# A two-layer decoder trunk on one core: one weight block's low part moves from VectorE to GpSimd, and its high part one place back on ScalarE

## The reference

```python
def one_block(args):            # forgetting attention
    sc = jnp.einsum('bqhd,bkhd->bhqk', qi, k) * scale
    sc = sc + ci[..., None] - logcum[:, :, None, :]
    sc = jnp.where(mask[None, None], sc, -jnp.inf)
    p = jax.nn.softmax(sc, axis=-1)
    return jnp.einsum('bhqk,bkhd->bqhd', p.astype(v.dtype), v)
...
y = jnp.concatenate([mix, mo], axis=-1) @ w_o[layer]
x = layer_norm(DN_ALPHA * x + y, ln_g[layer, 0], ln_b[layer, 0])
x = layer_norm(DN_ALPHA * x + sq_relu_mlp(x, w_up[layer], w_down[layer]),
               ln_g[layer, 1], ln_b[layer, 1])
```

## Time and profile before

| | |
|---|---|
| median of 3 runs | 1163.6 us (1163.14 to 1164.12) |
| profiled execution | 1163.3 us |
| its span, first to last instruction | 1161.6 us |
| TensorE busy | 1139.0 us, 98% |
| VectorE busy | 623.5 us, 54% |
| ScalarE busy | 487.4 us, 42% |
| GpSimd busy | 131.6 us, 11% |
| last forgetting step, units 0 to 7 on TensorE | about 734.6 to 751.8 us of the span |

### The profile page before, as it was taken

The page is one execution under the profiler, slowest core; times in us unless marked ns, Lnnn a source line. Parts: engine busy times, 40 slices in busy tenths (PEclk is TensorE's granted clock), DMA queues, the critical chain, the costliest instruction groups (busy, mean ns, idle before and its releaser), DMA issues.

```text
span 1161.6 us, 16344 instructions
## 1 busy us (share of the span) xinstructions
PE 1139.0 (98%) x5792; PEld 960.9 (83%) x5792; DVE 623.5 (54%) x1065; ACT 487.4 (42%) x843; POOL 131.6 (11%) x157
## 2 busy tenths in 40 slices
PE   8999999999999999999999999999999999999997
PEld 7888889888888888889778888788888888888886
DVE  6668766444223444355587787746454233444226
ACT  6556358343122343225765656537443212334120
POOL 5000054000000000233301101046000000000000
PEclk9999999999999999999999999999999999999999
DMA  8222323233333333332212222133233333333232
GB/s 308 77 73 91 100 65 109 74 106 92 103 97 91 92 105 93 103 96 82 65 39 71 55 55 72 41 105 92 80 100 95 105 90 90 91 92 106 91 112 88
DMA packets 163798, 107.22 MB, mean 92 GB/s; under 512 B 4642, under 2 KB 156194, under 8 KB 163620
## 3 DMA queue, kind: packets, MB, share of 16 engines
q1 hardware_dynamic: 163172, 104.18, 29.8%
q10 hardware_dynamic: 576, 2.36, 0.6%
HBM read 104.43 MB, written 2.10 MB: 92 GB/s over the span
## 4 chain that ended last, share of the span: by engine, by line
PE 85%; DVE 6%; ACT 4%; issue 2%; DMA 2%; POOL 1%; SPq 0%; DVEq 0%; ACTq 0%; POOLq 0%
PE proj L581 69%; PE pv L581 3%; PE sc L581 2%; PE proj L976 2%; PE sc L976 2%; PE pv L976 2%; PE tr L976 2%; PE tr L632 1%; DVE w_lo L1585 1%; ACT w_hi L1193 1%; DMA w_raw<-in_w_o 1%; PE proj L676 1%; DVE sc L1654 1%; DMA mem_raw<-in_mem 1%; ACT x L1376 0%
## 5 line engine op out<-in xcount | busy, mean ns | idle before, releaser
L581 PE MATMUL proj<-x_hi,w_hi 128*128 128x512 f32 (+1 forms) x752 | 291.7, 389 | 3.5 <-DVE w_lo L1585 1.6
L1585 DVE TENSOR_TENSOR w_lo<-w_raw,w_hi 128x1024 fp32r<-128x1024 f32 (+1 forms) x168 | 210.0, 1251 | 155.1 <-ACT w_hi L1193 107.1
L581 PE MATMUL proj<-x_hi,w_lo 128*128 128x512 f32 (+1 forms) x752 | 287.1, 383 | 0.0
L581 PE MATMUL proj<-x_lo,w_hi 128*128 128x512 f32 (+1 forms) x752 | 282.6, 383 | 0.0
L1193 ACT CAST w_hi<-w_raw 128x1024 fp32r<-128x1024 f32 x153 | 159.9, 1045 | 203.2 <-PE proj L581 199.6
L581 PEld LDWEIGHTS proj<-x_hi,w_hi 128*128 128x128 f32 x752 | 141.4, 188 | 31.2 <-ACT x_hi L1378 2.8
L581 PEld LDWEIGHTS proj<-x_hi,w_lo 128*128 128x128 f32 x752 | 141.3, 188 | 28.2
L581 PEld LDWEIGHTS proj<-x_lo,w_hi 128*128 128x128 f32 x752 | 139.2, 188 | 24.9
L581 PE MATMUL proj<-h_hi,w_hi 128*128 128x512 f32 (+1 forms) x384 | 146.4, 381 | 0.4 <-DVE w_lo L1585 0.4
L581 PE MATMUL proj<-h_hi,w_lo 128*128 128x512 f32 (+1 forms) x384 | 146.1, 380 | 0.0
L581 PE MATMUL proj<-h_lo,w_hi 128*128 128x512 f32 (+1 forms) x384 | 146.0, 380 | 0.0
(11 more groups left out here) (380 smaller groups left out, 1784.1 us busy)
## 6 DMA issues: line engine op xcount, KB each, us to landing
w_raw<-in_w_up SPq DMA_DIRECT2D x64, 512.0 KB, 4.0
w_raw<-in_w_down SPq DMA_DIRECT2D x64, 512.0 KB, 3.6
w_raw<-in_w_o SPq DMA_DIRECT2D x16, 512.0 KB, 3.6
w_raw<-in_a_w_in SPq DMA_DIRECT2D x12, 512.0 KB, 3.3
w_raw<-in_kv_w SPq DMA_DIRECT2D x12, 512.0 KB, 3.8
w_raw<-in_b_w_q SPq DMA_DIRECT2D x8, 512.0 KB, 3.7
w_raw<-in_mem_w_kv SPq DMA_DIRECT2D x5, 512.0 KB, 3.5
x<-in_x SPq DMA_DIRECT2D x4, 512.0 KB, 10.9
```

Source lines behind the costliest of these rows:

```text
L581: last = pe.matmul(target, lhs, rhs, start=start and n == 0, stop=stop and n == len(terms) - 1)
L1585: return dve.tensor_tensor(target, whole, hi.bitcast(F32), ALU.subtract)
```

## The change

Block 115's low part is made by GpSimd instead of VectorE. On ScalarE, the cast that makes its high part stands behind the exponential of unit 1 and no longer ahead of it. Since counts of `w_split` must come in order, GpSimd waits for block 114's count, and VectorE waits for block 115's before it makes block 116's low part. GpSimd's new instruction stands between the last `copy_heads` and the layer norm.

```diff
@@ scalar, pair_step @@
+                    if ahead(s):
+                        exponentials(s, u)
                     if late is not None and u == 1:
                         prepare(late)
-                    if ahead(s):
-                        exponentials(s, u)
                     if u >= 2:
                         turned_probs(s, u - 2)
@@ vector, pair_step @@
-                    if late is not None and u == 1:
-                        prepare(late)
                     if ahead(s):
                         if u + 1 < 8:
                             row_max(s, u + 1)
@@
                 if late is not None:
+                    dve.wait_ge(w_split, late.at(1))
                     prepare(Pos(LEAD_UNITS[1]))
@@ gpsimd @@
             for pair in range(PAIRS):
                 copy_heads(pair)
+            late = Pos(B_WO[1] + 1)
+            late_parts = weights(late)
+            pool.wait_ge(w_split, late.at())
+            pool.wait_ge(w_hi_ready, late.at(1))
+            pool.tensor_tensor(late_parts[1], raw(late), late_parts[0].bitcast(F32), ALU.subtract).then_inc(w_split, 1)
             layer_norm(2)
```

## The result

| | before | after |
|---|---|---|
| median of 22 runs each, us | 1163.98 (1163.01 to 1166.43) | 1166.2 (1165.02 to 1167.13) |
| ratio after to before | | 1.0017, 95% interval 1.0012 to 1.0023 |
| profiled execution, us | 1163.3 | 1166.98 |
| its span, us; mean granted clock | 1161.6; 0.998 | 1165.2; 0.996 |

The changed kernel is slower by 1.4 to 2.7 us by the interval, 2.0 in the middle. The forecast was 1.0, and the time lies above the range. By the bound of 0.2% it counts as the same.

A forecast was written before the change was run, and what follows sets the result against it. TensorE, busy 98% of the span, was taken as the bound. Block 115's first product 1.10 us late (0.91 won, 2.01 paid), less 0.10 given back, made +1.0: 1163.6 + 1.0 = 1164.6 us, range 1163.6 to 1165.7.

The forecast's parts named there:

- The relief: In front of unit 1's transposes in the last step: TensorE's 0.91 us wait goes, as unit 1's scaling runs earlier.
- What comes in its place: Block 115's later cast ends at 738.41; GpSimd starts at 738.5, takes 2.4 us, low part ready at 740.9.
- Who waits: TensorE at block 115's first product: starts at about 740.96 instead of 739.86, 1.10 us late.
- What is given back: At unit 2's transposes: 0 to 0.3 us comes back, 0.1 taken; the 0.40 us wait at 745.89 stays.
- Queues and the port: GpSimd's later sums, SP's load and VectorE's new wait cost nothing; unit 2's scaling waits for GpSimd's port, hidden.
- Rivals (a) to (d): (a) port collision, 1165.0 to 1165.5, 0.14; (b) relief decides, -1.0, 0.04; (c) slow GpSimd, +3.1, 0.05; (d) waits repaid, +0.4, 0.09.
- The clock: Behind TensorE's idle gap, growing from 0.91 to about 1.9 us: granted clock stays 1.00, no cost given.
- The base: Whole kernel: starting time of 1163.6 us, the median of the runs, to which +1.0 us was added.

The follow-up runs named there:

- the changed kernel with three products: The changed kernel plus three thrown-away 128x512 products on TensorE in front of block 115's first product; 1164.23 us, ratio 1.0007 to the kernel before.
- ScalarE's order with seven: The kernel before with only ScalarE's later cast, plus seven thrown-away 128x512 products in front of unit 1's transposes; 1165.05 us, ratio 1.0012.
- the later read: The changed kernel with two projections of block 114 ahead of the first two of block 115, read two units later; 1164.61 us, ratio 1.0007.
- the three filled kernels: Thrown-away TensorE products added: seven or three to the changed kernel (1164.68, 1164.23 us), seven to the kernel before with ScalarE's new order (1165.05 us).
- the one of 1.90: Stop in the kernel before with only ScalarE's order changed, block 115's cast behind unit 1's exponential, low part on VectorE; 1165.9 us, ratio 1.0018.

## Why the prediction was wrong

- **The relief.** It took the 0.91 us as gone and unit 1's scaling at 738.1 to 738.45. It ran at 738.35 to 738.70, less the 0.26 us of this execution 738.09 to 738.44. Right.
- **What comes in its place.** GpSimd was put at 738.5 with 2.4 us, low part ready at 740.9. It was 738.84 - 0.26 = 738.58 with 2.34 us, ready at 740.92. Right; the line through the two smaller tiles held, and so did the choice against the worst row.
- **Who waits.** Block 115 at 740.96 instead of 739.86, 1.10 us late. Measured 741.23 - 0.26 = 740.97, and +1.11, +1.11 and +1.12 into the step in the three profiled executions. The gap of 1.8 to 2.1 us ended by GpSimd is the 2.01. Right.
- **What is given back.** 0.1 of 0 to 0.3 was taken. In the execution without a fall, unit 2's transposes start 0.96 us behind block 115's first product (741.89 to 740.93) and before 1.24, so 0.28 came back there. But unit 3's transposes are 1.12 late again (9.66 us into the step instead of 8.54), the later wait on `pb_lo` grew from 0.40 to 0.56, and at the end of the step the delay is 1.10: nothing is given back. Off by 0.1. That this wait would not vanish was right; that it would keep its 0.40 was not.
- **Queues and the port.** SP's load went out at 741.34 and hurt nobody. Unit 2's scaling stood for GpSimd: 1.53 us, ending 0.21 behind GpSimd's end, forecast over 1 us and hidden. The lock of the Trainium skill (SBUF — State Buffer, Who interferes with whom) agrees: GpSimd, the first to start, kept its 2.34 us and VectorE paid it all. Rivals (a) to (d) did not come in the changed kernel: no collision with unit 1's scaling, GpSimd not slower, the waits not repaid.
- **The clock: the step that failed.** The prediction saw the idle gap grow from 0.91 to 1.9 us and said "I give the clock no cost", because products had gone on at their old lengths behind one gap of 1.57 us. A gap of 1.57 us was taken as a rule for a longer one. The gap of 1.57 us itself has no fall behind it in any of the 14 profiled executions, but that says nothing of 2.0 us. The runs show a fall of the clock behind the 2.0 us stop in two of three profiled executions, 1.29 and 1.23 us each. The term missing from the sum was this price times its chance. By the profiles that is two thirds of 1.26, 0.8 us. By the mean clocks it is 0.0011 less, 0.75 of a fall of 0.0015, so 0.9 us. 1.10 and 0.8 to 0.9 are 1.9 to 2.0: the 2.0 that was measured, and the 2.09 between the means (1166.20 and 1164.11).
- **The base.** The forecast time of 1164.6 is 1.6 below the measured 1166.2. Of this, 0.4 is no fault of the mechanism: it started from the 1163.6 of 3 runs, and 22 runs of the kernel before have 1163.98.

The Trainium skill (TensorE: Matmul & The Clock Gate, Part 1: The HAM clock gate) says that the lower level is the default and activity releases the higher one, and that the count of slow products at a kernel's start differs from run to run of the same kernel. The three executions above show such a difference in the middle of a kernel: the same stop of 2.0 us, twice with slow products behind it and once without. This would have been a reason to make the clock a rival with a chance of its own.

**What stays open.** The last step is not the only place where the clock falls. Eleven of the 14 profiled executions of all kernels have a fall that begins between 799 and 805 as well, and then run 405.0 to 405.6 us from the first product with `lead_hi` to the end; the three without it (of before, of the changed kernel with three products and of ScalarE's order with seven) take 404.4 to 404.5. The profile of before is thus a good execution, and the 3.6 us between the two first profiles overstates the change. This fall also limits what was said of stops. From 780 on, TensorE stands for 0.44 us at most ahead of it in every profile, with the fall (changed kernel) as without it (before):

```profile
803.10 0.38 PE L581 MATMUL proj<-x_hi,w_hi 128*128 128x256 f32 x1 [0.44 <-ACT x_hi L1378]
```

```profile
800.54 0.38 PE L581 MATMUL proj<-x_hi,w_hi 128*128 128x256 f32 x1 [0.44 <-ACT x_hi L1378]
```

In four of the eleven the clock is down clearly before this stop (with the later read at 800.6, the stop at 801.4). So a long stop is one way to lose the clock here, and there is another, whose cause was not looked for. Whether the later place of the step makes that fall likelier was not tried by itself; the three filled kernels, whose step ends 1.0 to 1.2 us late too, have mean clocks of 0.9977 to 0.9980, not below the 0.9973 of before. The mean clock is a coarse witness: it has three digits, and it counts a fall behind the last products too, which costs nothing. That, I think, is why the slope of 0.66 us per 0.001 is below the 0.9 which 1.29 us for 0.0015 would give, and why the changed kernel has +1.36 at equal clock where its rows have 1.10; neither was tested.

## What to carry to other kernels

Cost a wait on TensorE twice: by how late the next product is, and by what the stop may do to the clock behind it. Useless products in the stop can be worth their while if the wait can't be removed: here they took 1.4 us off the median. When work is handed to a slower engine, start it early enough that nobody waits, even if that means moving its inputs ahead too: the same GpSimd instruction lost 1.1 us in one place, and with it in another the step was 0.8 us shorter than before. Read more than one profiled execution, and the mean clock of all of them, before a difference of 2 us is put down to rows.

## What was not expected of the hardware

- A single stop of 2.0 us of a TensorE that is otherwise busy was followed by some 3.4 us at the 1.2 GHz level, within a microsecond of the restart (1.00 at 736 to 741, 0.50 at 742 to 745), and not in every execution. In the last step, stops of 0.91, 1.31, 1.40 and 1.65 us had none behind them in the profiled executions, nor had the one of 1.57 at 587 in any of 14. Nor had the one of 1.90, but the mean clocks of that kernel's other executions are as low as the changed kernel's.
- In 3.4 us at half the clock only 1.2 to 1.3 us were lost and not 1.7. One part is that products of 128x512 follow each other at 0.43 us there (743.53 to 743.96) and at 0.23 at the full clock (740.18 to 740.41 before), which is less than twice. In the third execution 0.22 of the rest is a wait that shrank (at `pb_lo`, 0.34 us where the one without a fall has 0.56), but in the first this wait stayed at 0.56 and the loss was still 1.29. What covers the rest is not settled.
- GpSimd's subtraction of 128x1024 takes 2.34 to 2.38 us in the last step and stretches VectorE's scaling of 128x384 from 0.42 to 1.53, and of 128x256 from 0.35 to 2.00 with the cast in its old place. Beside VectorE's last instructions of the step before it took 2.52.
